# Eight of the second layer's twelve modulation blocks summed by VectorE from unsplit weights, TensorE adding only the partitions

## The reference, cut to what matters

```python
s_lat = jax.nn.silu(c)
s_ctx = jax.nn.silu(c_ctx)
for l in range(2):
    mod = (s_lat @ ada_w[l] + ada_b[l])[:, None, :]       # ada_w[l]: 1024 x 6144
    sh1, sc1, g1, sh2, sc2, g2 = jnp.split(mod, 6, -1)    # six parts of 1024
    n_mod = 2 if last else 6                              # last is layer 1
    modc = jnp.split(s_ctx @ ada_w[l][:, :n_mod * 1024] + ada_b[l][:n_mod * 1024], n_mod)
    a_lat = rms_norm(h, norm1_g[l]) * (1 + sc1) + sh1
    a_ctx = rms_norm(hc, norm1_g[l]) * (1 + modc[1]) + modc[0]
    ...                                                   # mixer, then:
    h = h + g1 * y
    h = h + g2 * ffn(rms_norm(h, norm2_g[l]) * (1 + sc2) + sh2)
```

## Time and profile before

| | us |
|---|---|
| median of 3 runs | 2944.88 |
| lowest and highest | 2943.93, 2949.64 |
| span of the profiled execution | 2938.9 |
| between that span and the median | 6.0 |
| PE busy in the span | 2766.3 (94%) |
| DVE busy | 1832.5 (62%) |
| ACT busy | 1517.6 (52%) |
| POOL busy | 155.1 (5%) |

### The profile page before, as it was taken

How to read it: one execution, slowest core, us unless ns; L and a number is a source line. 1 busy time by engine, 2 the same in 40 slices (tenths; PEclk the granted TensorE clock), 3 DMA queues, 4 the chain that set the end, 5 groups by cost and what they waited for, 6 DMA issues and landing times.

```text
span 2938.9 us, 34671 instructions
## 1 busy us (share of the span) xinstructions
PE 2766.3 (94%) x13289; PEld 2282.2 (78%) x13289; DVE 1832.5 (62%) x2326; ACT 1517.6 (52%) x2155; POOL 155.1 (5%) x204
## 2 busy tenths in 40 slices
PE   6998899999998869999999899999699999998899
PEld 5777678878886558888888788787578888787787
DVE  5676665666677545545788855569655555546555
ACT  5563455545554224444677645574354455564453
POOL 2111000000030000000000000002000000100100
PEclk8999999999999869999999999999899999999999
DMA  7673256656662015555799855551055655551444
GB/s 269 229 249 99 69 193 211 219 196 222 223 188 65 1 58 179 158 179 175 270 320 334 305 165 172 173 186 43 24 182 165 209 186 168 205 180 43 136 157 143
DMA packets 266291, 510.45 MB, mean 174 GB/s; under 512 B 9268, under 2 KB 40204, under 8 KB 266139
## 3 DMA queue, kind: packets, MB, share of 16 engines
q1 hardware_dynamic: 262336, 498.11, 50.8%
q0 software_dynamic: 3808, 10.35, 1.2%
HBM read 507.33 MB, written 1.05 MB: 173 GB/s over the span
## 4 chain that ended last, share of the span: by engine, by line
PE 84%; DVE 8%; ACT 3%; DMA 2%; issue 1%; POOL 1%; ACTq 0%; DVEq 0%; SPq 0%; POOLq 0%
PE bank L416 23%; PE bank L417 23%; PE bank L420 22%; PE bank L1324 2%; PE bank L1337 2%; DVE wlo L324 2%; DVE h_hid L2571 1%; PE bank L1350 1%; PE bank L387 1%; ACT whi L320 1%; PE bank L389 1%; PE bank L388 1%; PE bank L2117 1%; PE bank L510 1%; DMA raw<-in_moe_w 1%
## 5 line engine op out<-in xcount | busy, mean ns | idle before, releaser
L324 DVE TENSOR_TENSOR wlo<-raw,whi 128x1024 fp32r<-128x1024 f32 (+1 forms) x1012 | 1195.6, 1199 | 785.6 <-ACT whi L320 781.1
L320 ACT ACTIVATE whi<-raw 128x1024 fp32r<-128x1024 f32 (+1 forms) x1012 | 1037.5, 1040 | 815.2 <-PE bank L420 771.5
L416 PE MATMUL bank<-whi,xhi 128*128 128x512 f32 (+2 forms) x2328 | 888.9, 382 | 22.2 <-DVE wlo L324 8.9
L420 PE MATMUL bank<-whi,xlo 128*128 128x512 f32 (+2 forms) x2328 | 879.2, 378 | 0.0
L417 PE MATMUL bank<-wlo,xhi 128*128 128x512 f32 (+2 forms) x2328 | 879.2, 378 | 0.0
L416 PEld LDWEIGHTS bank<-whi,xhi 128*128 128x128 f32 x2328 | 442.5, 190 | 107.4 <-issue 21.1
L420 PEld LDWEIGHTS bank<-whi,xlo 128*128 128x128 f32 x2328 | 441.8, 190 | 78.1
L417 PEld LDWEIGHTS bank<-wlo,xhi 128*128 128x128 f32 x2328 | 442.0, 190 | 74.7
L416 PE MATMUL bank<-whi,f_hhi 128*128 128x512 f32 x496 | 197.6, 398 | 3.1 <-ACT f_gates L971 3.1
L417 PE MATMUL bank<-wlo,f_hhi 128*128 128x512 f32 x496 | 196.6, 396 | 0.0
L420 PE MATMUL bank<-whi,f_hlo 128*128 128x512 f32 x496 | 196.4, 396 | 0.0
(11 more groups left out here) (532 smaller groups left out, 2892.4 us busy)
## 6 DMA issues: line engine op xcount, KB each, us to landing
raw<-in_ffn_w SPq DMA_DIRECT2D x180, 1024.0 KB, 5.1
raw<-in_moe_w SPq DMA_DIRECT2D x96, 1024.0 KB, 5.6
raw<-in_ada_w SPq DMA_DIRECT2D x48, 1024.0 KB, 6.2
raw<-in_moe_w SPq DMA_DIRECT2D x48, 768.0 KB, 4.7
raw<-in_ev_w_in SPq DMA_DIRECT2D x24, 1024.0 KB, 5.7
raw<-in_ffn_w SPq DMA_DIRECT2D x36, 512.0 KB, 3.6
raw<-in_hyb_w_in SPq DMA_DIRECT2D x18, 1024.0 KB, 5.0
raw<-in_attn_w_qkv SPq DMA_DIRECT2D x18, 1024.0 KB, 5.1
```

Source lines behind the costliest of these rows:

```text
L320: nc.scalar.activation(whole, part, ACT.Copy).then_inc(sem("w_hi"), 1)
L324: nc.vector.tensor_tensor(wlo[s][:, 0:rows, 0:n], part, whole.bitcast(F32), ALU.subtract)\
L416: nc.tensor.matmul(bank[:, 0:n], xk_h, whi[s][:, wk, 0:n], start=first, stop=False)
L420: ins = nc.tensor.matmul(bank[:, 0:n], xk_l, whi[s][:, wk, 0:n], start=False, stop=last)
```

## The change

In both passes only the first two pairs keep a chunk (chunks 0 to 3: parts 0 and 1, for both streams). The other four parts go two to each pass: parts 3 and 2 in the first, 4 and 5 in the second (`VEC_PARTS`). For a part, four loads of 2 x 128 rows by 1024 columns (1 MB) go into `vec_w`, which lies on `R_F["xe"]` and is one buffer; for each load VectorE does two instructions of 128 x 1024: weight times the silu value of its partition, added to a sum. After 4 loads that sum holds, in each of 128 partitions, an eighth of the terms. For parts 3 and 4 the sum lies in `y[:, 0, :]`, and TensorE adds the partitions with eight matmuls that have one column of ones (`vector_columns_pe`), in pair 4. For the gates the sum stays in `gates1`, whose row 0 starts with the bias and whose other rows start with zeros; the copy to `gates` now takes all 128 rows (1 MB), and `resid_pe` sums 128 rows with `ones` in place of 5. SyncE issues the loads in its queue of units: load 0 ahead of the unit at place 5, then one every three units, each after a wait for VectorE to be done with the load before it. VectorE does them beside steps 1, 4, 7, ... 22.

```diff
+    ssig = sb("ssig", [P, 2 * KD])
...
-            ld.columns(a["ada_w"][1], D, (first + j) * N, N)
+            for w, c0, k, width in [(w, j * N, k, n) for w in (w1, w3) for k in (0, 4)] + \
+                    [(a["ada_w"][1], (2 * st + j) * N, k, N) for k in (0, 4) if j < 2]:
+                if at >= VEC_FIRST and (at - VEC_FIRST) % VEC_EVERY == 0 and (at - VEC_FIRST) // VEC_EVERY < VECS:
+                    load_vector(ld, st, (at - VEC_FIRST) // VEC_EVERY)
+                ld.unit(tiles(w, k, 4, c0, width), 4, width)
+                at += 1
...
+    VECS, VEC_FIRST, VEC_EVERY = 8, 5, 3
+    VEC_PARTS = ((3, 2), (4, 5))
...
+    def load_vector(ld, st, i):
+        if i:
+            ld.after(f"vec{st}{i - 1}")
+        else:
+            ld.after("ff1:x" if st else "ff0:x")
+        src = tiles(a["ada_w"][1], i % 4 * 2, 2, VEC_PARTS[st][i // 4] * D, D)
+        ld.eng.dma_start(vec_w, src).then_inc(sem("vec_in"), 16)
+
+    def vector_dve(e, st, i):
+        e.eng.wait_ge(sem("vec_in"), 16 * (VECS * st + i + 1))
+        to = gates1[:, st, :] if i >= 4 else vec_sum
+        if i == 4 and st == 0:
+            loaded(e, "gates1 bias", 2)
+        for j in range(2):
+            k = i % 4 * 2 + j
+            if k == 0 and i < 4:
+                ins = nc.vector.tensor_scalar(to, vec_w[:, j, :], ssig[:, k:k + 1], None, ALU.mult)
+            else:
+                ins = nc.vector.scalar_tensor_tensor(out=to, in0=vec_w[:, j, :], scalar=ssig[:, k:k + 1], in1=to,
+                                                     op0=ALU.mult, op1=ALU.add)
+            e.link(ins, (f"vec{st}{i}", "vec") if j else None)
+
+    def vector_columns_pe(e, st):
+        e.after(f"vec{st}3", f"mod1 cols{2 * st + 1}")
+        for i in range(KD):
+            ins = nc.tensor.matmul(O[1][:, i:i + 1], vec_sum[:, i * P:i * P + P], ones[:, 0:1], start=True, stop=True)
+        e.put(ins, f"vec cols_ps{st}")
...
-            chunk_pe(e, f.s, first + j)
+            if j < 2:
+                chunk_pe(e, f.s, 2 * st + j)
...
-        e.after(f"mod1 row{first + CHUNKS - 1}")
+        e.after(f"vec cols{st}")
...
+        e.link(nc.gpsimd.memset(gates1[:, :, :], 0.0))
...
-        side_load(e, gates[0:5, :, :], gates1[0:5, :, :], "gates1")
+        side_load(e, gates[:, :, :], gates1[:, :, :], "gates1")
...
     def inside_ffn_dve(e, s, x, i):
+        if i % VEC_EVERY == 1 and i // VEC_EVERY < VECS:
+            vector_dve(e, int(x is IN_O0), i // VEC_EVERY)
```

More of the change, by code:

```diff
@@ L281, in unit, with after @@
             self.r.n += 1
+        def after(self, name):
+            if not plan["dry"]:
+                key, n = old[name]
+                self.eng.wait_ge(sem(f"{key}_done"), n)
         def columns(self, w, k, c0, n):
@@ new lines, in vector_columns_pe, with vector_columns_dve @@
+    def vector_columns_pe(e, st):
[3 more added lines that the diff above has]
+        e.put(ins, f"vec cols_ps{st}")
+    def vector_columns_dve(e, st):
+        e.after(f"vec cols_ps{st}")
+        part = VEC_PARTS[st][0]
+        e.link(nc.vector.tensor_tensor(mod1[:, column_part[part], :, 0], O[1][:, 0:KD], cols[:, 4, 8 * part:8 * part + KD],
+                                       ALU.add), f"vec cols{st}")
+        if st:
+            e.link(nc.vector.scalar_tensor_tensor(out=scal1[:, 1, :, 0], in0=mod1[:, 3, :, 0], scalar=1.0, in1=gain2(1),
+                                                  op0=ALU.add, op1=ALU.mult), "mod1")
@@ L950, in chunk_pe @@
     def chunk_pe(e, s, c):
[L952 to L955, removed]
+        if c >= 2:
+            e.after(f"mod1 cols{c - 2}", "vec cols0")
         for k0 in (0, 4):
@@ L967, in chunk_act @@
     def chunk_act(e, c):
-        part, c0 = c // 2, c * N % D
-        to = row1[0:4, c % 2, :] if has_columns(c) else gates1[0:4, part // 3, c0:c0 + N]
-        e.put(nc.scalar.activation(to, O[c % 2][0:4, :], ACT.Copy), f"mod1 row{c}")
+        e.put(nc.scalar.activation(row1[0:4, c % 2, :], O[c % 2][0:4, :], ACT.Copy), f"mod1 row{c}")
     def chunk_columns_dve(e, c):
@@ L1023, in gates1_pool @@
         e.after(*deps)
+        e.link(nc.gpsimd.memset(gates1[:, :, :], 0.0))
         for g, part in enumerate((2, 5)):
[L1025 removed]
+            side_load(e, gates1[0:1, g, :], a["ada_b"][1:2, part * D:part * D + D], "gates1 bias")
     def gates1_copy_pool(e):
[L1029 to L1031 removed]
+        e.after("res_f1:gate", "vec")
+        side_load(e, gates[:, :, :], gates1[:, :, :], "gates1")
         loaded(e, "gates1")
@@ L1037, in resid_pe @@
         e.after(*deps)
+        rows_ = 5 if pick_ is not None else P
         for c in range(2):
-            ins = nc.tensor.matmul(banks[c][:, :], pick_[0:5, :], gates[0:5, g, c * N:c * N + N],
-                                   start=True, stop=True)
+            ins = nc.tensor.matmul(banks[c][:, :], (ones if pick_ is None else pick_)[0:rows_, :],
+                                   gates[0:rows_, g, c * N:c * N + N], start=True, stop=True)
         e.put(ins, tag + ":gate")
@@ L3477, in _ @@
                 loaded(e, "gates1")
-                resid_pe(e, "res_o", pick_lat, 0)
+                resid_pe(e, "res_o", None, 0)
             if on(4):
```

66 lines of the change are left out of this document (34 added, 32 removed).

## The result

The changed kernel takes 2904.46 us (median of 4 runs, 2901.96 to 2906.21) against 2944.4 us of the kernel before (4 runs beside it); the ratio is 0.9863, 95% interval 0.9847 to 0.9878. The forecast was 2907, in a range from 2901 to 2919. It was faster, by some 40 us or 1.4%, and the interval stays clear of 1.

A forecast was written before the change was run, and what follows sets the result against it. The prediction took TensorE's work to bound the stage, with 36% of VectorE free. Savings of 25.2 + 13.25 + 3.9 - 3.9 = 38.4 us off the 2938.9 span, plus 6.0 around it, gave 2906.5, say 2907; range 2901 to 2919.

The forecast's parts named there:

- Chunks of pairs 2 to 4: Pairs 2, 3 and 4 of both passes: six modulation chunks leave TensorE, 4.2 us each, saving 25.2 us.
- The last chunk and its stop: Behind pair 5: chunk and TensorE's wait for ScalarE's copy go, saving 8.15 and 5.10 us, together 13.25.
- The rival by which the stop stays: Full DMA makes the second half of each pass start as late as before: 2912 us, chance 0.08.
- The columns: TensorE turns columns at two places fewer per pass, saving 3.9 us; one-column matmuls add 3.9, so they cancel.
- VectorE: Pieces of two instructions, 2.6 us, beside the units of both passes stay hidden: cost 0, up to 10 us.
- The rival of collisions: VectorE's pieces come between splits and TensorE, giving back 10 to 20 us: 2917 to 2927, chance 0.13.
- The loads: SyncE's 1 MB vector loads land in 6.2 us, about 9 us between issue and use: cost 0.
- The rival that ends slower than before: The single load buffer clocks the pass, VectorE holding splits behind late loads: 2987 us at 5 us a stop, chance 0.03.
- GpSimd: Gate copy grows from 40 KB to 1 MB before the odd layer's tables, 2.7 us of cover: 0 to 1.5 us.
- The sum: Whole kernel: 38.4 us off the span of 2938.9 gives 2900.5; with 6.0 around it 2906.5, say 2907.

The follow-up runs named there:

- narrow gates: Changed kernel with only 5 rows of the gate sums copied and summed (40 KB in place of 1 MB); passes of 212.21 and 205.24 us.

## Why the prediction was right

- **Chunks of pairs 2 to 4**, 25.2 us forecast. The pair that lost a chunk and its columns went from 27.84 to 22.66 us, as read ahead: right, and right to read the distance between starts and not the recorded duration of 0.39 us. The split of these 5.2 us was a little off. From pair 2 to pair 3 the changed kernel has the columns and no chunk, and takes 23.89 us: the columns cost 1.2 with their seams where the forecast had 0.98, and a chunk 4.0 where it had 4.2. Six chunks are thus 24.0 us.
- **The last chunk and its stop**, 13.25 us forecast. 8.16 + 5.12 = 13.28 measured; put back, it costs 22.61 - 15.09 = 7.5 and 5.0. The run with the later wait parts it: 4.3 us matmuls and seams in each pass, 3.9 and 0.8 the stop with its clock, where the prediction had 3.9 for the matmuls and 5.45 in all for the stops. The rival by which the stop stays (2912) is out.
- **The columns**, -3.9 + 3.9 us. Taken off are four times 1.2 us, 5.0 in all. A set of one-column matmuls took 1.68 us and not 1.96, 16 rows at 0.105. Pair 4, in which it stands, takes 21.90 us and not the 24.6 that the prediction wanted to see "across the ones": it forgot there that the distance from pair 4 to pair 5 is a short one (25.28 before, where the others had 27.84), since pair 5's first unit is half as wide. The sum did not use that number.
- **VectorE**, 0. A piece is 2.60 us, as estimated from 256 and 512 columns (1.281 us an instruction for 1.29). Left out altogether, it changes nothing. The rival of collisions is out at this size. Its price was real, though: with pieces of twice the size 6.0 us went, and the run took 2910.51. The Trainium skill (Vector Engine (DVE) Microarchitecture Reference, "Points that are easy to get wrong") says that scalar_tensor_tensor with two sources in SBUF that aren't bf16 has half the throughput. The trace agrees if the measure is an instruction with one source: tensor_scalar took 0.747 us for the same 128 x 1024, scalar_tensor_tensor 1.281; less the 212 ns that the prediction takes as fixed, these are 535 and 1069 ns, an estimate. It was no added cost here, because the row of 750 ns for 512 columns, from which the forecast was worked out, is such an instruction with two sources and had it in already.
- **The loads**, 0. They land in 5.4 us, VectorE does not wait, and the shortest time from issue to use is 9.6 us where the prediction counted about 9. The rival that ends slower than before has a real mechanism, but these loads have the lead that it denies them; with loads three places later it is there, at 6.1 us a load.
- **GpSimd**, 0 to 1.5. The copy grew by 1.8 us to 6.7, inside the 2.7 of cover, and cost nothing.
- **The sum.** The two passes gave 38.42 us against 38.4. That it fits to 0.1 us is in part luck: six chunks gave 1.2 us less than forecast, and the columns taken off 1.1 more. Outside the passes two errors nearly cancelled as well. The stretches with unchanged instructions came out 1.46 and 1.68 us longer and the rest 0.92 shorter, 2.2 us in all, and 6.0 us were added around the span where 1.8 belong: the profiled execution of before was one of the faster ones. So the forecast of 2906.5 stands 4.2 - 2.2 = 2 us above the profiled 2904.5. That is less than the runs of before differ among themselves (2941.16 to 2949.64), so the last 2 us say nothing for or against the forecast.

## What to carry to other kernels

Price an edit on a full engine by the distance between starts of like places with and without the thing, and look for the same structure elsewhere in the kernel that already does without it: that gave both passes to 0.1 us here, though the parts of the sum were off by up to 1.2. Look at the one stop of the stage apart; here a copy queued behind a late split, with a wait on it ahead of the next phase, cost 3.9 us with the slow clock behind it, and a later wait, with the result in a bank that nobody needs so soon, removed it. For work given to an engine with room ask two things: whether its load stays below the time of each pair, not only on average over the pass, and whether a single piece fits between two deadlines of that engine. Here pieces of 2.6 us were free, pieces of 5.2 us cost 3.0 us a pass at two places, and pieces of 7.8 us failed both tests.

## What the runs showed of the hardware

TensorE need not stand still for its granted clock to fall. A lump of 24 matmuls of one column, 48 recorded rows back to back, counts as busy all through, and yet the granted clock fell in it to 0.50, 1.2 GHz. Split into three of 1.68 us (at 479.72, 497.87 and 503.41 us) the same matmuls leave it at 1.00, and each pass is 4.0 us shorter.

The gate matmuls at the end of a pass (four recorded rows of 0.48 us, which sum 5 rows of the gate) are a place where the clock differs from run to run under the same instructions. With narrow gates it is 0.57 in the 4 us behind those that precede the first pass, and 0.83 over 582 to 592 us, around those that end it:

```profile
376.00:380.00 4.00, 4.00 (x12) 3.12 (x11) 1.61 (x3) 0.37 (x2) 0.00 (x0) 0.57 0.76 261
...
582.00:592.00 10.00, 10.00 (x33) 6.84 (x32) 7.80 (x12) 2.19 (x3) 0.00 (x0) 0.83 0.88 305
```

In the changed kernel's profile both stretches are at 1.00. The first fall makes the first pass 1.6 us longer (212.21 against 210.58), the second lies behind the end of the first pass and makes the second one 1.5 longer (205.24 against 203.73). The same step is in the second passes of the two runs with the last chunk back (0.61 and 0.58 in the 4 us behind the gate matmuls). TensorE counts as busy in all these places; why the clock falls in some profiles and not in others stays open.

The +1.46 and +1.68 us of the table above do not need the change. The kernel before with its sixth chunk moved has the instructions of before in both stretches and takes 373.0 and 234.3 us there, and the second profile of the changed kernel takes 373.06 and 234.43. Over all kernels the stretch in front of the passes took 372 to 375 us and the one behind them 232.8 to 239.0, with no order that follows the edits.
